# Decoder step on one core: the second half of a gate weight is asked for after the first four row gathers, and the first weight sum stands after the second tile's combination

## The reference, cut to what matters

```python
    combine = jnp.sum(jax.nn.one_hot(expert_id, N_EXPERTS, dtype=f32) * w_top[..., None], axis=-2)
    ...
    for e in range(N_EXPERTS):
        gu = jnp.einsum('bld,df->blf', u, w_gate_up[e])
        hid = jax.nn.silu(gu[..., :D_EXPERT]) * gu[..., D_EXPERT:]
        moe = moe + combine[..., e:e + 1] * jnp.einsum('blf,fd->bld', hid, w_down[e])
    h = h + moe

    u = rmsnorm(h, norm_ple)
    gate = jax.nn.sigmoid(jnp.einsum('bld,de->ble', u, w_ple_gate))
    h = h + gate * jnp.einsum('blp,pd->bld', p_l, w_ple_proj)
    ...
    y_prompt = rmsnorm(hp, norm_final)
```

## Time and profile before

| | |
|---|---|
| median of 3 runs | 825.62 us (825.39 to 827.02) |
| time of the profiled execution | 829.97 us |
| its span, first to last instruction | 828.1 us |
| PE busy | 808.1 us (98%) |
| DVE busy | 403.3 us (49%) |
| ACT busy | 215.5 us (26%) |
| POOL busy | 152.3 us (18%) |
| DMA moved | 135.23 MB, mean 163 GB/s |

### The profile page before, as it was taken

One profiled execution on the slowest core, in us unless ns is written; L12 is line 12 of the kernel. 1 busy time (PEld: TensorE's weight loads), 2 busy tenths in 40 slices (PEclk: granted clock), 3 DMA queues, 4 the chain that ended last, 5 costly groups with the idle time before them and its releaser, 6 DMA issues. The chain is left out here.

```text
span 828.1 us, 12897 instructions
## 1 busy us (share of the span) xinstructions
PE 808.1 (98%) x5184; PEld 507.7 (61%) x5184; DVE 403.3 (49%) x882; ACT 215.5 (26%) x470; POOL 152.3 (18%) x182
## 2 busy tenths in 40 slices
PE   9999999999999999999999999999999999999995
PEld 4545777887879987677777776455433333334442
DVE  3223357584667512664864457836352101104975
ACT  3211152229234410131101110122121111114376
POOL 0143222004046133300220034000100001004100
PEclk9999999999999999999999999999999999999998
DMA  9520364321111020404232222234899999996211
GB/s 360 207 101 1 110 203 153 85 88 58 54 48 58 19 85 14 195 21 161 102 144 76 86 102 104 78 125 180 302 402 363 420 428 421 409 389 193 70 51 64
DMA packets 20976, 135.23 MB, mean 163 GB/s; under 512 B 2436, under 2 KB 3076, under 8 KB 13748
## 3 DMA queue, kind: packets, MB, share of 16 engines
q1 hardware_dynamic: 13472, 103.34, 32.0%
q0 software_dynamic: 4720, 23.83, 7.9%
q10 hardware_dynamic: 2724, 7.21, 2.6%
HBM read 118.94 MB, written 19.63 MB: 167 GB/s over the span
## 5 line engine op out<-in xcount | busy, mean ns | idle before, releaser
L817 PE MATMUL pair<-mem 128*128 128x288 f32 x640 | 158.9, 408 | 0.0
L817 PEld LDWEIGHTS pair<-mem 128*128 128x128 f32 x640 | 120.3, 190 | 35.6 <-ACT mem L1507 2.1
L987 PE MATMUL single<-mem 128*128 128x288 f32 x448 | 110.0, 407 | 0.3
L987 PEld LDWEIGHTS single<-mem 128*128 128x128 f32 x448 | 84.7, 190 | 25.7 <-issue 1.6
L1374 PE MATMUL single<-mem 128*32 128x512 f32 x768 | 85.1, 594 | 0.9 <-DVE mem L2532 0.9
L1507 ACT ACTIVATE mem<-pair 128x512 f32<-128x512 f32 (+5 forms) x83 | 36.5, 487 | 163.8 <-PE pair L817 63.1
L1507 ACT ACTIVATE mem<-single 128x256 f32<-128x256 f32 (+5 forms) x109 | 44.6, 419 | 127.0 <-PE single L1235 48.5
L1374 PEld LDWEIGHTS single<-mem 128*32 128x32 f32 x768 | 23.6, 110 | 52.8 <-issue 51.7
L2525 DVE SCALAR_TENSOR_TENSOR mem<-single,mem 128x256 f32<-128x256 f32 x12 | 5.8, 485 | 102.3 <-PE single L1374 91.1
L1226 PE MATMUL pair<-mem 128*128 128x512 f32 x112 | 51.0, 601 | 0.0
L1443 PE MATMUL pair<-mem 128*128 128x512 f32 x112 | 49.4, 595 | 0.3 <-DVE mem L2593 0.3
(11 more groups left out here) (431 smaller groups left out, 1121.7 us busy)
## 6 DMA issues: line engine op xcount, KB each, us to landing
mem<-in_w_gu SPq DMA_DIRECT2D x17, 2048.0 KB, 14.8
mem<-in_w_down SPq DMA_DIRECT2D x17, 1024.0 KB, 13.8
y_slots<-mem SPq DMA_DIRECT2D x9, 512.0 KB, 11.1
y_slots<-in_zeros POOLq DMA_DIRECT2D x8, 512.0 KB, 7.9
mem<-in_w_ga SPq DMA_DIRECT2D x2, 2048.0 KB, 8.4
mem<-in_w_gb SPq DMA_DIRECT2D x2, 2048.0 KB, 7.8
mem<-in_w_wo SPq DMA_DIRECT2D x2, 2048.0 KB, 7.8
mem<-in_w_pg SPq DMA_DIRECT2D x2, 2048.0 KB, 18.0
```

What stands on the lines that cost most here:

```text
L817: last = nc.tensor.matmul(pb[:, hf, 0:HALF], w(k), rhs[:, k, hf * HALF:(hf + 1) * HALF], start=(k == 0), stop=(k == kk - 1))
L987: last = nc.tensor.matmul(single[plan.buf[s]][:, 0:HALF], lhs[:, k, :], rhs[:, k, :], start=(k == 0 and j in (0, 1, 3, 4)), stop=(k == 3), ...
```

## The change

On SP the transfer of `w_pg[1]` is moved behind the loop over further overflow blocks (which is not entered in this execution) and waits for three things: `ga01` and `ga11`, the two gathers of tile 1, which are the third and the fourth gather, and the landing of `w_pg[0]`. On PE the first product waits for `w_pg[0]` alone. On DVE `weights_1`, with its wait for both halves, moves from ahead of `combine(0)` to behind `combine(1)`.

```diff
             sp.wait_ge(sem("gu_mm"), NPH)
-            sp.dma_start(w_pg[1], a["w_pg1"].rearrange("k p c -> p k c")).then_inc(sem("w_pg"), 16)
             with sp.If(n_ov > 1):
...
+            sp.wait_ge(sem("ga01"), 16)
+            sp.wait_ge(sem("ga11"), 16)
+            sp.wait_ge(sem("w_pg"), 16)
+            sp.dma_start(w_pg[1], a["w_pg1"].rearrange("k p c -> p k c")).then_inc(sem("w_pg"), 16)
             sp.wait_ge(sem("h3"), 2)
             sp.wait_ge(sem("w_pg"), 32)
             sp.dma_start(nfin, a["norm_final"]).then_inc(sem("w_pg"), 16)
@@
                 pe.wait_ge(sem("u3T"), 4 * q + 1)
-                pe.wait_ge(sem("w_pg"), 32)
+                pe.wait_ge(sem("w_pg"), 16)
                 pe.wait_ge(sem("pp"), 4 + q)
@@
-            weights_1()
             combine(0)
             u3_evac(0)
             combine(1)
+            weights_1()
             r3(0)
             u3_evac(1)
             rows_1(0)
```

## The result

| | before | changed |
|---|---|---|
| median of 5 runs | 826.05 us (825.39 to 827.02) | 835.92 us (834.44 to 837.12) |
| time of the profiled execution | 829.97 us | 836.88 us |
| its span | 828.1 us | 835.0 us |

The ratio is 1.011, with a 95% interval of 1.0097 to 1.0124: slower by 9.9 us. The forecast was slower by 4.6 us with a range that ended at 833.2 us, so direction and place were right and the size was not.

The account below looks back on a forecast made before the run. Tail bound by transfers until 757.89, then by equal PE and DVE chains. Tile 2's transpose 4.1 us late plus 0.5 for the clock: 4.6 us slower, median 825.62 to 830.2 us; 8-in-10 range 826.7 to 833.2.

Parts of the forecast that it names:

- The store lands earlier: Experts' last store: with 2 MB less in the queues it lands at 746.05 for 747.87, 1.8 us earlier.
- The gather's issue is held by the weight sum: First gather's issue: held until DVE's weights_1 ended; with that sum gone, it falls from 2.48 us to 0.94.
- the 1.54 us: First gather's issue: the time forecast to be saved with DVE idle; bound from below nothing.
- The load of 9.6 us: Second weight half, issued at 756.8 beside tile 2's gathers: takes 9.6 us, landed at 766.4; bounds 7.8 and 10.7.
- the gathers of later tiles are issued against the same combinations as before: Later tiles' gathers: listed among the items that cost nothing.
- The wait and what is behind it: DVE waits 5 us at weights_1 until 766.4; tile 2's transpose starts 4.1 us late, at 779.05.
- the landing less 762.3: General form of the tail's loss: L, when the second weight half lands, less 762.3.
- The early fourth gather: Fourth gather: issued at 750.58, lands 6.2 us later at 756.8, for 760.2 before.
- The clock: PE idle 4.5 us ahead of p5: clock may fall to 1.2 GHz, costing 0 to 0.9 us, 0.5 taken.
- its window 8 to 10: Kernel's first microseconds: 3 128 x 512 instructions in 2 us, later 6; basis for 2.2 us lost at half pace.
- The one that would have made it faster: Weights arrive before they are missed, L 762.3 or less: tail early by PE's 1.66 us, 824.0 us; chance 0.07.
- The clock rival: Clock stays low through p5 and p6, ending at 784.7, 9.8 us behind: 835.4 us; chance 0.06.

Follow-up runs that it names:

- gathers held: Changed kernel with the gathers of tiles 2 to 4 held on POOL until the second weight half has landed: 832.29 us, ratio to before 1.0075.
- 16 KB rows: Changed kernel with the second weight half laid out so each partition's 16 KB are one row; same bytes, order and waits: 831.08 us, ratio 1.0068.
- both: Changed kernel with 16 KB rows for the second weight half and the gathers of tiles 2 to 4 held until it has landed: 829.83 us, 1.0038.
- the second profile of before: Kernel before, unchanged, run and profiled once more: median 826.52 us, ratio 1.0008; its profiled execution took 825.77 us.
- the run with PE filled: Changed kernel with nine unread 128 x 512 products on PE between p2 and p5: 836.18 us, ratio 1.012.
- the run with the SP and PE parts: Changed kernel with the weight sum back ahead of the first combination, SP and PE parts kept: 840.53 us, ratio 1.016.
- tiles 3 and 4 held: Changed kernel with only the gathers of tiles 3 and 4 held until the second weight half has landed: 834.17 us, ratio 1.0097.

## Why the prediction was right or wrong

**The store lands earlier: right in size, by another transfer than the one priced.** 1.8 us were forecast; the last store lands 6.76 - 5.10 = 1.7 us earlier behind the experts' end. But it is the overflow block's 128 KB, issued 0.80 us behind the 512 KB store that the prediction priced at 4.2 us. In three runs with the same edit on SP (gathers held, 16 KB rows, both) that 512 KB store took 2.8 to 2.9 us, so it no longer came last. A price too high and a last store that was overlooked cancel, and that is luck. The first gather then starts 0.26 us behind the landing and not 0.81, half a microsecond that was not foreseen.

**The gather's issue is held by the weight sum: right as a mechanism.** 0.95 us was measured, and the hold followed the sum to another gather when only the sum was moved (2.75 us). Every held issue ended 0.8 us behind DVE's instruction: 0.82 and 0.78 in the first profile, 0.81, 0.83. The Trainium skill, page "SBUF — State Buffer", section "Who interferes with whom", infers that a `tensor_tensor` does not hold descriptor generation; the 2.75 us here, for 0.94, disagree. But the 1.54 us was the price in one execution: in the second profile of before, whose execution was closer to the median, the hold is 0.3 us, a fifth of what I wrote down.

**The load of 9.6 us: this is the step that failed.** It took 14.35, outside its bounds of 7.8 to 10.7. Three faults add up to the 4.75 us. The bounds took the price alone from a load of 16 KB rows (7.8); this one has 2 KB pieces, and takes 9.2 alone: 1.4 us. Tile 2's gathers cost 2.4 us and not 1.8: 0.6 us. And tile 3's gathers, issued at 758.99 and 760.23, were left out of the sum, though the prediction has tile 1 combined at 761.4, inside its own load: 2.8 us. Its sentence "the gathers of later tiles are issued against the same combinations as before" put them at nothing; it is true of when they are issued, and leaves out that the load is now in flight beside them. The form and the order of the gathers stood in the diff and the program. And the one row of this very transfer, asked for at 730.91 and landed just before 748.05, is 17.1 us beside other transfers; it shows that 10.7 us, a row of another form, was no upper bound.

**The wait and what is behind it: right.** The loss was put at the landing less 762.3, that is, less 21.19 us behind the experts' end. The landing was 29.03 behind it, so 7.8 us; tile 2's combination ended at 780.48, 41.60 behind the experts' end for 33.79, 7.8 us later. The early fourth gather (14.52 us behind the experts' end for 19.05) gave 1.1 us more than forecast (0.4 from the start of its issue, 0.8 from a landing of 5.42 us for 6.2), and the load took it all back.

**The clock: right that it falls, under-sized.** 0.5 us was taken, from a range of 0 to 0.9. The clock was low for 5.2 us of p5 and p6, which cost 2.6 us (9.71 for the 7.11 of the run with PE filled), and PE ended 782.07 - 780.48 = 1.6 us behind DVE. That excess cannot be put down to the length of the wait. After a wait of only 4.18 us, less than the 4.5 that were forecast, the clock was low for 6.2 us in the run with held gathers and PE ended 2.05 us behind DVE; after 4.09 us with 16 KB rows it came back after 2.8 us, and PE was 0.4 us behind. What decides when it comes back, no run here shows. The prediction's price was also no row of the low clock: in its window 8 to 10 the granted clock is 1.00. That its loss of 2.2 us is near the 2.6 is luck.

**Sum in the profile:** 7.8 + 1.6 = 9.4, for 43.19 - 33.84 = 9.35. Against the forecast of 4.6: the load adds 4.75 and the clock 1.1, the early gathers take 1.1 off. That the runs show 9.9 fits with both profiled executions: before's had 1.6 us more in the tail than the second profile, and the changed kernel's own lay 1.0 us above its median. Where that 1.0 us lay is not shown.

**Rivals.** None of them happened. The one that would have made it faster needed a load of 7.8 us among other things; in the table it takes both edits, large rows and no gathers, to get there, and even then the landing comes 23.28 us behind the experts' end, 2.1 us too late (829.83 us). The clock rival's 835.4 us stands near the measured time by accident: it had the load landing at 766.4 and p5 and p6 taking 14 us, and neither came.

## What to carry to other kernels

Price a moved transfer by its form and by everything that will be in flight until it lands, not only when it starts: the same 2 MB took 7.7, 9.2, 9.8 or 14.35 us, and 17.1 in its old place. A transfer that was asked for early costs only what it delays; asked for late, it needs its whole duration as slack, so first look whether it can be cut, so that only the part used last goes late. And before a gain of a microsecond is built on one profile, compare that execution's own time with the median, and profile the same kernel twice.

## What the runs showed of the hardware

- Size of pieces and sharing compound in a load of 2 MB: 2 KB pieces cost 1.5 us over 16 KB rows alone, and 4.6 us beside gathers of 4 KB rows.
- The same transfer under full DMA engines landed in 17.1 us in one execution and 16.0 in another of the same kernel.
- An indirect DMA's issue on GpSimd that meets a wide DVE `tensor_tensor` with both operands in SBUF ends 0.8 us after it, where it takes 0.94 us by itself: 2.48, 1.96, 2.75 and 1.25 us in the rows shown.
- TensorE's clock fell to 1.2 GHz in each of the seven waits of 2.9, 4.1, 4.2, 6.0, 8.7, 12.8 and 13.2 us, between 2.2 us (the run with the SP and PE parts) and 4.4 us (tiles 3 and 4 held) after the last product: 3.7 us in the changed kernel, 2.7 us in the run with rows and held gathers (p2 ended at 766.16, and a mean of 0.71 puts the fall at 768.84). In the wait of 1.7 us of before, and with unread products in the wait, it stayed at 2.4 GHz. It came back 2.8 to 6.2 us after the work did, and not later after the longer waits: 2.8 us after the wait of 4.1, 6.2 after 4.2, 5.2 after 8.7. The window of the fall in the run with rows and held gathers:

```profile
768.00:770.00 2.00, 0.92 (x1) 0.50 (x2) 1.97 (x3) 0.00 (x0) 1.63 (x2) 0.71 0.69 170
```
